# A gather of routed rows in a two-layer MoE trunk: rows sorted by stream and expert, and the slot ranks of pair 0 by two products

## The reference, cut to what matters

```python
scores = sigmoid(hf @ router_w)                   # 256 tokens x 16 experts
biased = scores + router_bias
best_group = argmax(sum of the top 2 of biased in each group of 4 experts)
top_idx = top 2 of biased inside the best group   # 2 experts per token
gates = scores at top_idx, divided by their sum
act = silu(hf @ w_gate[e]) * (hf @ w_up[e])       # 1024 -> 512, for each expert e
y = sum over e of (act * gate[e]) @ w_down[e]     # 512 -> 1024
x = x + g2 * y
```

## Time and profile before

| | us |
|---|---|
| median of three runs | 1069.12 (1066.43 to 1071.21) |
| the profiled execution | 1067.82 |
| its span | 1066.0 |
| PE busy | 988.6 (93%) |
| expert stage of layer 0, from its first gate and up product | 319.03 to the next layer's first norm product at 549.29 |
| expert stage of layer 1 | 829.69 to the end |

### The profile page before, as it was taken

How to read it: one execution, slowest core, us unless ns; L and a number is a source line. 1 busy time by engine, 2 the same in 40 slices (tenths; PEclk the granted TensorE clock), 3 DMA queues, 4 the chain that set the end, 5 groups by cost and what they waited for, 6 DMA issues and landing times.

```text
span 1066.0 us, 13634 instructions
## 1 busy us (share of the span) xinstructions
PE 988.6 (93%) x5114; PEld 587.2 (55%) x5114; DVE 347.9 (33%) x946; ACT 224.4 (21%) x492; POOL 102.0 (10%) x82
## 2 busy tenths in 40 slices
PE   4899999998989999999899999899898999899987
PEld 2348876665866443443254588777586553344333
DVE  2116113782361132332160421248635202222224
ACT  1213223421012211111041222342201221111111
POOL 0000004641100000000000000066310000000000
PEclk9899999999999999999999999999999999999999
DMA  9965333159998799999998524240877779999992
GB/s 391 427 267 191 124 139 114 65 210 428 403 365 357 303 423 414 382 421 422 424 423 351 211 109 158 79 159 1 326 286 292 316 305 423 423 363 422 421 422 112
DMA packets 36835, 316.38 MB, mean 297 GB/s; under 512 B 4192, under 2 KB 4336, under 8 KB 5168
## 3 DMA queue, kind: packets, MB, share of 16 engines
q1 hardware_dynamic: 35856, 311.21, 71.6%
q0 software_dynamic: 928, 4.47, 1.0%
HBM read 313.82 MB, written 1.85 MB: 296 GB/s over the span
## 4 chain that ended last, share of the span: by engine, by line
PE 72%; DMA 14%; DVE 7%; ACT 3%; issue 2%; SPq 1%; ACTq 0%; DVEq 0%
PE ps L918 17%; DMA ring<-w_gu 11%; PE ps L499 11%; PE ps L606 8%; PE ps L930 7%; PE ps L799 5%; PE ps L875 3%; DMA ring<-w_in 3%; PE ps L785 3%; PE ps L891 3%; PE ps L624 3%; PE ps L717 2%; PE ps L479 2%; PE ps L512 1%; PE ps L655 1%
## 5 line engine op out<-in xcount | busy, mean ns | idle before, releaser
L918 PE MATMUL ps<-ring,tmq 128*64 128x512 f32 x928 | 213.9, 602 | 19.9 <-DMA ring<-w_gu 18.4
L918 PEld LDWEIGHTS ps<-ring,tmq 128*64 128x64 f32 x928 | 68.0, 139 | 146.4 <-issue 124.3
L499 PE MATMUL ps<-more,ring 128*128 128x256 f32 x512 | 114.3, 381 | 0.5 <-ACT more L987 0.5
L930 PE MATMUL ps<-ring,tmq 128*64 128x512 f32 x512 | 113.4, 595 | 0.0
L499 PEld LDWEIGHTS ps<-more,ring 128*128 128x128 f32 x512 | 96.1, 190 | 15.5 <-issue 2.5
L987 ACT ACTIVATE tmq<-ps 128x256 f32<-128x256 f32 (+3 forms) x124 | 56.0, 465 | 218.2 <-PE ps L930 91.3
L606 PE MATMUL ps<-ring,more 128*128 128x512 f32 (+1 forms) x256 | 99.1, 548 | 1.6 <-DMA ring<-w_in 1.6
L1687 DVE TENSOR_TENSOR tmq<-tmq,ps 128x256 f32<-128x256 f32 x32 | 13.5, 421 | 214.3 <-ACT tmq L1224 214.3
L606 PEld LDWEIGHTS ps<-ring,more 128*128 128x128 f32 x256 | 48.8, 192 | 50.6 <-issue 46.5
L930 PEld LDWEIGHTS ps<-ring,tmq 128*64 128x64 f32 x512 | 35.3, 137 | 66.6 <-issue 66.3
L1698 DVE SCALAR_TENSOR_TENSOR x<-ps,mod,x 128x128 f32<-128x128 f32 x256 | 67.6, 341 | 1.9 <-PE ps L875 1.9
(11 more groups left out here) (234 smaller groups left out, 1009.1 us busy)
## 6 DMA issues: line engine op xcount, KB each, us to landing
ring<-w_gu SPq DMA_DIRECT2D x116, 1024.0 KB, 13.3
ring<-w_down SPq DMA_DIRECT2D x64, 1024.0 KB, 12.9
ring<-w_ada SPq DMA_DIRECT2D x24, 2048.0 KB, 12.6
ring<-w_in SPq DMA_DIRECT2D x16, 2048.0 KB, 17.9
ring<-w_out SPq DMA_DIRECT2D x4, 2048.0 KB, 12.3
more<-w_gu SPq DMA_DIRECT2D x8, 1024.0 KB, 13.5
cst<-consts SPq DMA_DIRECT2D x2, 2048.0 KB, 27.3
ring<-w_pa SPq DMA_DIRECT2D x2, 2048.0 KB, 8.4
```

The source lines that it names most:

```text
L499: mm = pe.matmul(ps[:, 5, i * NT:(i + 1) * NT], w[:, k, m * P:(m + 1) * P], h[:, k, :], start=k == 0, stop=k == KT - 1)
L918: mm = pe.matmul(ps[r:r + SLOTS, half, :].rearrange("p (j n) -> p j n", j=2), hg[:, k, r:r + SLOTS], gu_unit(l, kh, e, in_more)[:, :, kk, ...
L930: mm = pe.matmul(ps[r:r + SLOTS, 2 + n, :], at_[:, k, r:r + SLOTS], down_unit(l, k // 2)[:, e, k % 2, n * 512:(n + 1) * 512], start=k == 0 ...
```

## The change: what it does

**Two products instead of the list position (pair 0).** The rank of a token among those of its expert is now read directly as the slot: the product with the earlier tokens, and the count of stream 0 added for stream 1. The scan `before_e`, the product that added it and the product that gave the starts are gone, and so are the minimum and the subtraction of the window start on VectorE. Of the three VectorE operations that finish `h2tok` one stays ahead of `posm`, the other two come behind the one-hot matrices; TensorE's gather writes to banks 2 and 3 instead of 4 and 5, and waits for `h2tok` half by half.

**Rows by stream and expert.** The 512 rows now stand as 256 of stream 0, sorted by expert, and 256 of stream 1. A chunk of 128 rows then holds tokens of one stream only, so each of its products contracts over that stream's 128 tokens alone. `gg` has no stream index any more. The starts of the experts in each stream come from two scans on VectorE, behind `npass`.

**Windows in two parts.** The rows of one expert are now in two places. ScalarE copies 64 rows from its place in stream 0 to the window, and then 64 rows from its place in stream 1 to the same window, shifted by the number of rows of stream 0 (`window_at[2]`). So `hg` has 128 slots for each expert, of which the products read the first 64; `starts` holds three numbers for each expert. A pair needs six register loads and four copies, where it needed two and two. In pair 0 the six loads stand behind the first copy to `at_`, ahead of the second and of the sorted rows.

```diff
-                pe.wait_ge(sel_ready, 2 * l + 1)
+                pe.wait_ge(sel_ready, l + 1)
                 pe.matmul(ps[:, 1, 64:64 + 2 * NE], C("before"), rs[:, 0:2 * NE], start=True, stop=False)
-                pe.matmul(ps[:, 1, 64 + NE:64 + 2 * NE], ones, sel[:, 0, :], start=False, stop=False)
-                pe.wait_ge(sel_ready, 2 * l + 2)
-                pe.matmul(ps[:, 1, 64:64 + 2 * NE]..., ones, before_e..., start=False, stop=True)
-                mm = pe.matmul(ps[:, 1, 96:96 + NE], ones, before_e, start=True, stop=True)
-                mm.then_inc(pos_mm, 1)
-                for s in range(S):
-                    mm = pe.matmul(ps[:, 0, 128:128 + NE], ones, sel[:, s, :], start=s == 0, stop=s == 1)
+                pe.matmul(ps[:, 1, 64 + NE:64 + 2 * NE], ones, sel[:, 0, :], start=False, stop=True).then_inc(pos_mm, 1)
+                pe.matmul(ps[:, 0, 128:128 + 2 * NE], ones, rs[:, 0:2 * NE], start=True, stop=True).then_inc(pos_mm, 1)
...
-                                for s in range(S):
-                                    mm = pe.matmul(ps[:, 4 + 2 * (c % 2) + b, j * P:(j + 1) * P],
-                                                   h2tok[:, s, k * P:(k + 1) * P], gg[:, s, c * P:(c + 1) * P],
-                                                   start=s == 0, stop=s == 1)
+                                mm = pe.matmul(ps[:, 4 + 2 * (c % 2) + b, j * P:(j + 1) * P], h2tok[:, c // 2, k * P:(k + 1) * P],
+                                               gg[:, c * P:(c + 1) * P], start=True, stop=True)
...
-                                                   hg[:, k, r:r + SLOTS],
+                                                   hg[:, k, e, 0:SLOTS],
...
+                def window_starts(pr):
+                    return [[act.value_load(starts[0:1, bass.ds(pr * 2 + (j * NE + e), 1)], min_val=0, max_val=top)
+                             for j, top in enumerate((ROWS, ROWS, SLOTS))] for e in range(2)]
+
+                def windows(q, at):
+                    act.wait_ge(m_gu[l][1], q + 1)
+                    for e in range(2):
+                        copy(hg[:, :, e, 0:SLOTS], window_rows(at[e][0])).then_inc(m_hg[l], 1)
+                    for e in range(2):
+                        act.wait_ge(m_hg[l], q * 4 + e + 2)
+                        copy(hg[:, :, e, bass.ds(at[e][2], SLOTS)], window_rows(at[e][1])).then_inc(m_hg[l], 1)
...
-                        elif half == 0 and not first:
-                            windows(q + 1, pr + 1)
+                        elif half == 0 and first:
+                            act.wait_ge(m_starts[l], pss + 1)
+                            act.sem_inc(m_begun, 1)
+                            second = window_starts(pr + 1)
+                        elif half == 0:
+                            windows(q + 1, window_starts(pr + 1))
                     if first:
                         sorted_rows(pss)
-                        act.wait_ge(m_starts[l], pss + 1)
-                        act.sem_inc(m_begun, 1)
-                        windows(q + 1, pr + 1)
+                        windows(q + 1, second)
...
-                dve.tensor_tensor_scan(before_e[:, 1:NE], sel[:, 0, 0:NE - 1], sel[:, 1, 0:NE - 1], 0.0, ALU.add,
-                                       ALU.add).then_inc(sel_ready, 1)
                 ada_bias(*tail(l)[0])
-                for half, s in ((0, 1), (1, 0), (1, 1)):
-                    token_rows_of(half, s)
+                token_rows_of(0, 1)
...
-                link(dve.tensor_scalar(window_at, ps[:, 1, 96:96 + NE], float(LAST_WINDOW), None, ALU.min))
-                link(dve.tensor_tensor(posm, at_rows, rows(window_at, [P, S, NE]), ALU.subtract))
-                link(dve.scalar_tensor_tensor(posm, posm, 1.0, sel, ALU.add, ALU.mult))
+                link(dve.scalar_tensor_tensor(posm, slot, 1.0, sel, ALU.add, ALU.mult))
...
                 ins.then_inc(m_rowhot[l], 1)
+                for s in range(S):
+                    token_rows_of(1, s)
                 ada_bias(*tail(l)[1])
-                dve.tensor_copy(rowpos, at_rows)
-                dve.tensor_copy(base, ps[:, 1, 96:96 + NE])
                 dve.wait_ge(pos_mm, 2 * l + 2)
-                dve.tensor_reduce(sm[:, 8:9], ps[:, 0, 128:128 + NE], AX, ALU.max).then_inc(m_act[l], 1)
+                dve.tensor_copy(rowpos, slot)
+                link(dve.tensor_copy(counts, count))
+                link(dve.tensor_tensor(both[:, 0, 0, :], counts[:, 0, :], counts[:, 1, :], ALU.add))
+                dve.tensor_reduce(sm[:, 8:9], both[:, 0, 0, :], AX, ALU.max).then_inc(m_act[l], 1)
```

More of the change, by code:

```diff
@@ L68 @@
 ROWS = 2 * NT
-LAST_WINDOW = ROWS - SLOTS
 PAIRS = NE // 2
@@ L422, in _ @@
                     if l and ORDER[n] == (l, "gates", 0):
-                        sp.wait_ge(m_hg[l - 1], passes * (2 * PAIRS) + 3)
+                        sp.wait_ge(m_hg[l - 1], passes * (4 * PAIRS) + 5)
                         sp.dma_start(cst[:, C_LATE:CW], consts[:, C_LATE:CW]).then_inc(in_d, 16)
@@ L1636, in _ @@
                 dve.tensor_copy(npass[0:1, l:l + 1], sm[0:1, 12:13]).then_inc(routed, 1)
-                dve.tensor_copy(starts[0:1, :], window_at[0:1, :]).then_inc(m_starts[l], 1)
+                for s in range(S):
+                    ins = dve.tensor_tensor_scan(base[:, s, 1:NE], counts[:, s, 0:NE - 1], zeros[:, 0:NE - 1], float(s * NT),
+                                                 ALU.add, ALU.add)
+                link(ins)
+                dve.tensor_copy(window_at[:, 0:2, :], base)
@@ L1638, in _ @@
+                dve.tensor_copy(left, counts[:, 0, :])
+                dve.tensor_scalar(window_at[:, 2, :], counts[:, 0, :], float(SLOTS), None, ALU.min)
+                link(dve.tensor_tensor(rowpos, rowpos, base, ALU.add))
+                dve.tensor_copy(starts[0:1, :], qin[0:1, S * NE:S * NE + 3 * NE]).then_inc(m_starts[l], 1)
+                link(dve.tensor_tensor(rowpos[:, 1, :], rowpos[:, 1, :], counts[:, 0, :], ALU.subtract))
                 link(dve.tensor_tensor(both, rt[:, 3:5, :, :], rowpos.unsqueeze(1).to_broadcast([P, 2, S, NE]), ALU.mult))
-                link(dve.tensor_reduce(token_rows.rearrange("p (a s) -> p a s", a=2), both, AX, ALU.add))
@@ L1709, in shift @@
                         ins.then_inc(m_shift[l], 1)
-                        dve.wait_ge(m_shift[l], pss * 6 + done[0])
-                    dve.wait_ge(m_hg[l], pss * (2 * PAIRS) + (2 * PAIRS + 1))
-                    shift(dve.tensor_scalar(base, base, float(SLOTS), None, ALU.add))
-                    shift(dve.tensor_scalar(window_at, base, float(LAST_WINDOW), None, ALU.min))
-                    dve.tensor_copy(starts[0:1, :], window_at[0:1, :]).then_inc(m_starts[l], 1)
-                    shift(dve.tensor_tensor(posm, rowpos, rows(window_at, [P, S, NE]), ALU.subtract))
-                    shift(dve.scalar_tensor_tensor(posm, posm, 1.0, sel, ALU.add, ALU.mult))
-                    shift(dve.tensor_tensor(both[:, 0, :, :], rowpos, rows(base, [P, S, NE]), ALU.is_ge))
-                    shift(dve.tensor_tensor(posm, posm, both[:, 0, :, :], ALU.mult))
+                        dve.wait_ge(m_shift[l], pss * 7 + done[0])
+                    own, other, behind = (window_at[:, j, :] for j in range(3))
+                    dve.wait_ge(m_hg[l], pss * (4 * PAIRS) + (4 * PAIRS + 1))
+                    shift(dve.tensor_scalar(left, left, float(SLOTS), None, ALU.subtract))
+                    shift(dve.tensor_scalar(posm, posm, float(SLOTS), None, ALU.subtract))
+                    shift(dve.tensor_scalar(own, own, float(SLOTS), float(ROWS), ALU.add, ALU.min))
+                    shift(dve.tensor_scalar(other, left, -1.0, 0.0, ALU.mult, ALU.max))
+                    shift(dve.tensor_tensor(other, other, base[:, 1, :], ALU.add))
+                    shift(dve.tensor_scalar(other, other, float(ROWS), None, ALU.min))
+                    shift(dve.tensor_scalar(behind, left, 0.0, float(SLOTS), ALU.max, ALU.min))
+                    dve.tensor_copy(starts[0:1, :], qin[0:1, S * NE:S * NE + 3 * NE]).then_inc(m_starts[l], 1)
                 with dve.Fori(0, passes) as pss:
```

90 lines of the change are left out of this document (44 added, 46 removed).

## The result

The changed kernel takes 1053.31 us (median of 4 runs, 1050.77 to 1054.01), against 1069.86 for the kernel before beside it: ratio 0.9846, 95% interval 0.9816 to 0.9875. Forecast were 1052, from 17.1 us of gain; it is 16.5 us.

What follows compares the result with a forecast made beforehand. Bound: TensorE's path from the router's choice to pair 2's first weight transfer, then weight transfers. 2 x (1.72 + 6.14) + 1.35 = 17.1 us off 1067.8 gives 1050.7, with the median 1.3 above: 1052, own range 1047 to 1057, chance 0.68.

Steps and rivals of the forecast that it cites:

- Routing chain: From the router's choice over VectorE to the gather: one-hot matrices and gather 1.72 us earlier a layer, bounds 0.7 to 2.0.
- Hidden by 1.3 us: Hand-over to the experts: number of passes ready at 315.7, ScalarE's copy of the gather ending at 317.0, so no cost.
- Clock: Gathers: TensorE's idle shrinks, so half a clock fall instead of one over both layers, 1.35 us saved, bounds 2.7 to -2.7.
- Sort: Pair 0's row sort: half the instructions, 8.15 us instead of 14.29 with a 1.0 us wait, saving 6.14 us a layer.
- The whole 7.86 us arrive: Transfers at pair 2's first unit: TensorE still later by 1.1 us, so routing and sort gains pass on in full.
- The steady pairs: Later pairs: second copy to at_ ends at 377.5, wanted at 377.93, so six loads and four copies are hidden by 0.4 us.
- the price of 0.43 to 0.69 us a load: ScalarE's register loads for the windows: at least 0.43 and at most 0.69 us each with arithmetic, taken as 0.6.
- The rival on the slower side: Second at_ copy makes ScalarE bound each pair: slower from 3.4 us lateness, given 16 us slack; 1080 us, chance 0.06.

Runs made afterwards that it cites:

- e1: Changed kernel with TensorE's seven semaphore increments moved from behind its reading of the number of passes to ahead of the gather: 1052.25 us, ratio to before 0.9847.
- e4: Kernel before with two of three VectorE operations of 512 columns moved behind the one-hot matrices, gather in banks 2 and 3 waiting by halves: 1063.45 us, ratio 0.9962.
- e9: Changed kernel with VectorE's two operations of 512 columns put back ahead of the position: 1057.72 us, ratio to before 0.9903.
- e8: Kernel before with eight unread 128x128 products put into TensorE's idle 2 us ahead of the gather: 1063.95 us, ratio 0.9955.
- e2: Changed kernel with ScalarE's six register loads at the head of every pair instead of behind the first copy to at_: 1052.25 us, ratio to before 0.9846.
- e3: Changed kernel with each of the sort's 32 products issued twice, giving the former 128 instructions: 1062.59 us, ratio to before 0.9952.
- e12: Kernel before, unchanged, profiled once more to look at its gathers: 5.45 and 6.72 us.
- e11: Kernel before, unchanged, profiled again to look at its two gathers: 5.45 and 6.57 us.
- e7: Changed kernel in which SP starts pair 2's down units only when pair 2's fourth unit has landed: one execution, 1060.62 us.
- e6: Changed kernel with the six register loads done twice in pairs 1 to 7: 1075.93 us, ratio to before 1.0063.

## Why the prediction was right, and where its terms were off

**Routing chain, 1.72 us a layer.** The gather came 1.80 us earlier. In this term the hand-over to the experts was the step that failed: "Hidden by 1.3 us" compared the number of passes with ScalarE's copy, but behind that number TensorE's sequencer needs 2.7 us more (315.49 to 318.15), of which e1 took away 1.0. Before, TensorE read it at 316.16, while it was still working through the queued gather, and was ready 0.5 us ahead of ScalarE. About 0.9 us a layer were lost (5.69 and 5.47 us from the gather's start to the first product, less 4.64 before): the term is 0.8 instead of 1.72, and e4, which has only the reordering, shows the same by itself.

**Clock, 1.35 us.** Under-sized. The single profile had one slow gather in two; five of six are slow, and none of the 14 behind 0.83 us in the changed kernel and its variants. That makes 3.9 us. The totals agree roughly: e9 4.4 us less 0.6 of chain and e4 5.4 less 1.6 by the medians, both 3.8 (5.5 and 2.5 by the ratios), and 5.0 in e8, with its earlier start. So it is about 4 us. What it hangs on was right in the main, the idle ahead of the gather (e8), with the exception in e4.

**Sort, 6.14 us a layer.** On TensorE's path it was right: 64 instructions, 7.15 us, and a hole of 0.81 us from the register loads (e2 removes it), and pair 2's first unit moved by 6.1 us. At the end 9.3 us of 12.3 arrive by the medians of e3, 9.9 in the profiles. "The whole 7.86 us arrive" is the sentence that was too strong. From pair 1's first start to the landing of pair 3's fourth unit took 90.2 and 90.9 us before, and takes 86.3 and 83.8: 3.9 and 7.1 us less where 6.1 were expected. In layer 0, 16.65 units had moved by then, in layer 1 16.24, before 16.32 and 16.46, so the landing is late when more of the later units has moved ahead of it. That is not the change's alone: layer 0 of e12, the kernel before, has 16.65 units and 92.0 us. Over the profiles, twelve layers with the sort of 14.3 us (before, e3, e4, e8, e11, e12) take 89.8 to 92.0 us, 90.6 on average, and six with that of 8.3 (changed, e1, e9) 83.8 to 86.3, 85.4 on average: 5.2 us less. What sets the share of later data is open; e7 didn't settle it. The other part is the clock behind waits for weights. In the changed kernel's profile four runs of 32 instructions take 8.5 to 8.8 us instead of 7.1, in those of before two, three and three. The waits themselves are no longer than before (17.6 us in all and at most 2.7, where 18.4 and 2.7 were), and why the clock fell behind some of them is open.

**Sum.** 1.6 (chain) + 3.9 (clock) + 9.3 to 11.3 (sort) = 14.8 to 16.8 us, against 16.5 measured with an interval of some 3 us either way; undone parts need not add up exactly. The forecast's 3.4 + 1.35 + 12.3 had the chain 1.8 us too large, the clock 2.5 too small and the sort 1 to 3 too large. That these errors nearly cancel is luck.

**The steady pairs.** Right to a tenth of a microsecond (margin 0.4 us), and so is the price of 0.43 to 0.69 us a load: in pair 1 the six loads start 0.62 us apart (364.01 to 367.11), in pair 0 0.53. The load alone took 0.271 to 0.302 us in 96 of them. The Trainium skill's floor of about 600 ns for a `tensor_load` (DMA: Bandwidth & Descriptors, section "Latency and other measured facts"), weighed in the prediction, agrees here only with pair 1's whole step of 0.62 us, the arithmetic included.

**The rival on the slower side** did not come, but its threshold was wrong: e6, with 2.4 us of lateness a pair on average, is slower than before, where 3.4 had been worked out. The slack must be read from TensorE's waits for weights and not from the difference of the periods. The profile before had them already, 9.2 us a layer where 16 were worked out (both layers: us in total, times, longest):

```profile
PE ps L918 <- DMA ring<-w_gu: 18.4, 9, 2.7
```

## What to carry to other kernels

When a chain is shortened, follow each engine's sequencer to its next instruction: here a semaphore increment cost TensorE 0.15 us and a register load cost ScalarE 0.53 to 0.62 us as soon as the data were ready early, and both could be moved ahead of the wait. An idle of TensorE just ahead of dense work is dearer than it looks in one profile; count the slow instances over several executions before the clock is priced. And where transfers take over later in the stage, take slack from the measured waits.

## What the runs showed of the hardware that was not expected

With eight products of 128x128 that nobody reads in an idle of 2 us ahead of each gather, the kernel took 5.0 us less (e8), and both gathers took 3.82 us, where five of six had 5.45 to 6.72 before, mostly at a granted clock of 1.2 instead of 2.4 GHz. By the gathers that is worth 3.9 us. The Trainium skill, TensorE: Matmul & The Clock Gate, section "HAM oscillation — how this bites in real kernels", describes such falls for waits on DMA; here, by the rows above, they also follow a wait for a few small VectorE operations.
